# Scores of an attention branch with the query's two float halves stacked on the partitions

## The reference, cut to what matters

```python
def swa_sink_attention(q, k, v, sinks):
    qc = q.reshape(b, nc, CHUNK, A_KV_HEADS, g, d)
    kb, vb = chunk_band(k, n_prev), chunk_band(v, n_prev)
    logits = jnp.einsum('bnqhgd,bnkhd->bnhgqk', qc, kb) * (d ** -0.5)
    logits = jnp.where(valid[None, :, None, None, None, :], logits, -jnp.inf)
    probs = jax.nn.softmax(jnp.concatenate([logits, sink], axis=-1), axis=-1)[..., :-1]
    out = jnp.einsum('bnhgqk,bnkhd->bnqhgd', probs, vb)
```

## Time and profile before

| | us |
|---|---|
| median of three runs (lowest, highest) | 1487.55 (1487.49, 1489.11) |
| the profiled execution's own time | 1488.57 |
| its span, first to last instruction | 1486.6 |
| TensorE products busy | 1473.5, 7022 instructions |
| TensorE weight loads busy | 1215.9 |
| VectorE busy | 975.7 |
| ScalarE busy | 665.9 |
| score products of branch A (lines 662 to 664) | 26.9, 96 instructions |

### The profile page before, as it was taken

One profiled execution on the slowest core, in us unless ns is written; L12 is line 12 of the kernel. 1 busy time (PEld: TensorE's weight loads), 2 busy tenths in 40 slices (PEclk: granted clock), 3 DMA queues, 4 the chain that ended last, 5 costly groups with the idle time before them and its releaser, 6 DMA issues.

```text
span 1486.6 us, 19540 instructions
## 1 busy us (share of the span) xinstructions
PE 1473.5 (99%) x7022; PEld 1215.9 (82%) x7022; DVE 975.7 (66%) x1614; ACT 665.9 (45%) x1140; POOL 45.1 (3%) x35
## 2 busy tenths in 40 slices
PE   8999999999999999999999999999999999999998
PEld 6888888888888888888878888888888888888886
DVE  7777666565687734776477876665647776357753
ACT  6655555444444422443475555544345443234434
POOL 0000000002100000000200000000030000000001
PEclk9999999999999999999999999999999999999999
DMA  6222222232332233332432222222333332333331
GB/s 231 88 83 71 85 71 73 71 93 78 128 99 91 83 99 110 99 93 71 134 116 89 66 86 78 65 78 80 98 103 95 99 95 82 101 105 98 99 105 66
DMA packets 42560, 139.61 MB, mean 94 GB/s; under 512 B 5364, under 2 KB 5492, under 8 KB 42232
## 3 DMA queue, kind: packets, MB, share of 16 engines
q1 hardware_dynamic: 41760, 137.13, 29.3%
q10 hardware_dynamic: 728, 1.52, 0.3%
HBM read 136.53 MB, written 2.10 MB: 93 GB/s over the span
## 4 chain that ended last, share of the span: by engine, by line
PE 96%; ACT 1%; DVE 1%; DMA 1%; issue 1%; ACTq 0%; SPq 0%; DVEq 0%
PE dense L630 28%; PE dense L632 28%; PE dense L631 28%; PE turned L695 2%; PE branch L722 1%; PE dense L875 1%; PE dense L874 1%; PE dense L873 1%; DMA h<-in_x 1%; PE scores L683 1%; PE scores L682 1%; PE branch L708 1%; PE scores L686 0%; ACT tmp L1093 0%; ACT whi L943 0%
## 5 line engine op out<-in xcount | busy, mean ns | idle before, releaser
L630 PE MATMUL dense<-hg,whi 128*128 128x512 f32 x1376 | 547.7, 398 | 3.0 <-DVE hg L1285 2.6
L632 PE MATMUL dense<-hg,wlo 128*128 128x512 f32 x1376 | 537.4, 391 | 0.0
L631 PE MATMUL dense<-hg,whi 128*128 128x512 f32 x1376 | 537.0, 390 | 0.0
L943 ACT ACTIVATE whi<-raw 128x1024 fp32r<-128x1024 f32 (+3 forms) x269 | 265.4, 987 | 439.1 <-PE dense L632 417.5
L1272 DVE TENSOR_TENSOR wlo<-raw,whi 128x1024 fp32r<-128x1024 f32 (+3 forms) x269 | 305.9, 1137 | 180.2 <-ACT whi L943 177.9
L630 PEld LDWEIGHTS dense<-hg,whi 128*128 128x128 f32 x1376 | 259.6, 189 | 58.3 <-issue 4.8
L632 PEld LDWEIGHTS dense<-hg,wlo 128*128 128x128 f32 x1376 | 258.8, 188 | 55.0
L631 PEld LDWEIGHTS dense<-hg,whi 128*128 128x128 f32 x1376 | 259.4, 189 | 51.7 <-issue 1.0
L630 PE MATMUL dense<-act,whi 128*128 128x512 f32 x528 | 207.2, 393 | 0.0
L632 PE MATMUL dense<-act,wlo 128*128 128x512 f32 x528 | 205.6, 389 | 0.0
L631 PE MATMUL dense<-act,whi 128*128 128x512 f32 x528 | 205.5, 389 | 0.0
(11 more groups left out here) (188 smaller groups left out, 1269.8 us busy)
## 6 DMA issues: line engine op xcount, KB each, us to landing
raw<-in_w_up SPq DMA_DIRECT2D x88, 512.0 KB, 3.5
raw<-in_w_gate SPq DMA_DIRECT2D x48, 512.0 KB, 3.5
raw<-in_w_in SPq DMA_DIRECT2D x35, 512.0 KB, 3.5
raw<-in_w_down SPq DMA_DIRECT2D x32, 384.0 KB, 3.0
raw<-in_w_out SPq DMA_DIRECT2D x16, 512.0 KB, 3.4
raw<-in_w_down SPq DMA_DIRECT2D x16, 320.0 KB, 2.9
raw<-in_w_down_last SPq DMA_DIRECT2D x10, 512.0 KB, 3.5
raw<-in_w_br_a SPq DMA_DIRECT2D x8, 512.0 KB, 3.4
```

The source lines that it names most:

```text
L630: mm(out, a, xhi, start=start, stop=False)
L631: mm(out, a, xlo, start=False, stop=False)
L632: return mm(out, b, xhi, start=False, stop=stop)
L943: fn(whi[:, s, 0:cols], raw[:, r, 0:cols], ACT.Copy).then_inc(w_hi.sem, 1)
```

## The change

The first branch goes over to the stacked form. For each of a pair's two heads, `qa_st(g, s)` now holds the high half on the 64 partitions of head s and the low half on the other 64. The key is stored for each key head with the same 64 rows on both halves of the partitions, hi and lo, without zeros, by the "k" items that branches B and C have. A step is, for each key head s, two products of 128 columns (stacked q with k hi, stacked q with k lo), four in all, each head writing its own 128 columns of the bank. The first group of `SPLIT_QK` has eight items (four of q, four of k) in place of four, the second four in place of two, all of 64 partitions and 512 columns. All four partial products are now summed, lo x lo too.

```diff
-SPLIT_QK = [[("qa", 0, 0, 0), ("qa", 1, 0, 0), ("ka", 0, 0, 0), ("ka", 0, 1, 0)], [("qa", 2, 0, 0), ("qa", 3, 0, 0)]]
+SPLIT_QK = [[("qa", c, s, s) for c in range(2) for s in range(2)]
+            + [("k", 0, s, to) for s in range(2) for to in (s, 1 - s)],
+            [("qa", c, s, s) for c in range(2, 4) for s in range(2)]]
...
-    return SPLIT_QK[p][j:j + 1] if p < GROUPS else []
+    return SPLIT_QK[p][j:j + 1] if 0 < p < GROUPS else []
...
-        def qa_st(g, part):
-
-            return act2[:, 2 * g + part].rearrange("p i n -> p (i n)")
-
-        def qa_rows(p, part):
-
-            return qa_st(p // 2, part).rearrange("p (c i n) -> p c i n", i=2, n=CHUNK)[:, :, p % 2, :]
+        def qa_st(g, s):
+
+            return act2[:, 2 * g + s].rearrange("p i n -> p (i n)")
+
+        def qa_rows(p, s, r):
+
+            return qa_st(p // 2, s).rearrange("p (c i n) -> p c i n", i=2, n=CHUNK)[r, :, p % 2, :]
...
-                b = pair(bank_s[i % 2][:, 0:2 * P])
                 k0 = window(c)
-                q_hi, q_lo = [qa_st(g, part)[:, c * P:(c + 1) * P] for part in range(2)]
-                k_hi, k_lo = [ka_st[:, :, part, k0:k0 + P] for part in range(2)]
-                mm(b, q_hi, k_hi, start=True, stop=False)
-                mm(b, q_hi, k_lo, start=False, stop=False)
-                mm(b, q_lo, k_hi, start=False, stop=True).then_inc(scores.sem, 1)
+                for s in range(2):
+                    b, a = bank_s[i % 2][:, s * P:(s + 1) * P], qa_st(g, s)[:, c * P:(c + 1) * P]
+                    mm(b, a, ka_st[:, s, 0, k0:k0 + P], start=True, stop=False)
+                    last = mm(b, a, ka_st[:, s, 1, k0:k0 + P], start=False, stop=True)
+                last.then_inc(scores.sem, 1)
...
                 if kind == "qa":
-                    fn(qa_rows(c, 0), q[:, c, :].rearrange("p (c n) -> p c n", n=CHUNK), ACT.Copy).then_inc(qk_hi.sem, 1)
-                elif kind == "ka":
-                    fn(ka_st[:, s, 0, :], k[:, 0, :], ACT.Copy, scale=own_half[:, s:s + 1]).then_inc(qk_hi.sem, 1)
+                    fn(qa_rows(c, s, r), q[r, c, :].rearrange("p (c n) -> p c n", n=CHUNK),
+                       ACT.Copy).then_inc(qk_hi.sem, 1)
...
                 if kind == "qa":
-                    ve.tensor_tensor(qa_rows(c, 1), q[:, c, :].rearrange("p (c n) -> p c n", n=CHUNK),
-                                     qa_rows(c, 0).bitcast(F32), ALU.subtract).then_inc(qk_lo.sem, 1)
-                elif kind == "ka":
-                    ve.scalar_tensor_tensor(out=ka_st[:, s, 1, :], in0=k[:, 0, :], scalar=own_half[:, s:s + 1],
-                                            in1=ka_st[:, s, 0, :].bitcast(F32),
-                                            op0=ALU.mult, op1=ALU.subtract).then_inc(qk_lo.sem, 1)
+                    other = slice((1 - s) * HD, (2 - s) * HD)
+                    ve.tensor_tensor(qa_rows(c, s, other), q[r, c, :].rearrange("p (c n) -> p c n", n=CHUNK),
+                                     qa_rows(c, s, r).bitcast(F32), ALU.subtract).then_inc(qk_lo.sem, 1)
```

## The result

The changed kernel takes 1495.30 us (median of 6, 1494.16 to 1498.05), the kernel before beside it 1487.97 (median of 6, 1487.49 to 1489.11): a ratio of 1.0050, 95% interval 1.0039 to 1.0062, or 7.3 us between the medians. The profiled execution took 1495.56.

The account below looks back on a forecast made before the run. TensorE, busy 99% of the span, was taken as the bound; layer 0 at 4.5 and layer 1 at 2.15 us gave +6.6 on 1487.55, so 1494.1 us. The 8-in-10 range was 1491.3 to 1496.8.

Parts of the forecast that it names:

- Products: In 32 branch A steps, four products of 128 columns at 0.114 us, set by weight loads, replace three of 256: +2.5 us.
- Splits: Before step 0, eight VectorE low halves at 0.72 us each stop TensorE: +3.1 us in layer 0, +0.87 in layer 1.
- Rival (a): Before step 0, all eight splits cost 0.60 us, cheaper than held: sum +4.6, 1492.1 us; chance 0.10.
- (b): The splits before step 0 are covered and only the products count: +2.5, 1490.0 us; chance 0.05.
- (c): Columns set a product's price, so A steps shrink by 0.11 to 0.13 us: sum +1.4, 1489.0 us; chance 0.06.
- (d): TensorE is freed in the 32 A steps, at 0.11 us a step: -3.6, 1484.0 us; chance 0.02.
- Rival (e): The clock falls to 1.2 GHz in layer 0's stall of 3.1 us: +2.6 on top, 1496.7 us; chance 0.09.
- dense products of 0.63 behind the stall: Sign that the forecast is wrong: dense products behind layer 0's stall last 0.63 us, where elsewhere they last 0.39.
- What is late next: Work queued behind the splits moves later: unit 9's low-half weights come 3.5 us later in layer 0, TensorE's wait grows 0.1.
- The wait before unit 9: TensorE's wait in layer 0 for unit 9's low-half weights, 0.36 us before, forecast to grow by 0.1, between 0.3 and 0.6.
- nearly: In layer 1, unit 9's weights land at 801.0 and TensorE arrives at 801.3: no wait, but nearly.

Follow-up runs that it names:

- six-product kernel: The kernel before with each branch A score product of 256 columns cut into two of 128, splits untouched: 1497.39 us, ratio 1.0062.
- reordered list: The changed kernel with the first group's eight split items reordered so that more neighbours start in the same half: 1494.73 us, ratio 1.0045.
- filled stop: The changed kernel with 13 unread products of 512 columns before TensorE's wait at layer 0's first score step: 1495.11 us, ratio 1.0043.
- both edits: The changed kernel with its eight splits reordered and ScalarE's high halves issued before the forget branch's in unit 6: 1492.32 us, ratio 1.0028.
- two wide products: The changed kernel with two score products of 256 columns a step in place of four of 128: 1490.28 us, ratio 1.0016.

## Why the prediction was right, and where it was not

The time of 1495.3 lies 1.2 above the forecast and inside the range. Of the 1.2, 0.4 is the kernel before itself (1487.97 here, 1487.55 in the runs shown before), and 0.7 the change (7.3 for 6.6).

**Products.** Right: the number of loads and not of columns sets the price. More loads for the same columns cost 9.1 us, fewer gave 0.17 a step back. That it is the load, and not another price of each product that follows the clock, is likely from the rows and not shown by itself. The term came out at 2.4 for 2.5: 0.09 to 0.11 for steps followed by dense products (forecast 0.10), some 0.07 for the rest (0.075). The Trainium skill, "TensorE: Matmul & The Clock Gate", section "LDWEIGHTS (loading the stationary operand)", gives P/1.2 ns for P columns of weights, worked out 107 ns for 128, and all 64 of L664, 0.11 apart, agree; its "Back-to-back issue gap" would have them 56 ns apart (some 81 in a stream of loads and products), which the 128 products of L664 and L665 in the six-product kernel, at 275 to 277 ns and 0.11 apart, do not show either.

**Splits.** Right, to 0.02 us: 0.72 each by their neighbours' halves, a stop of 3.09 in layer 0, where there was no slack, and 0.85 in layer 1, where there were 2.35 us. Rival (a), all eight at 0.60, is excluded by the list's own distances, and the reordered list shows both prices in one row of eight. Rivals (b), (c) and (d) fell with these two.

**The clock.** This is the step that failed. Rival (e) happened, at a chance of 0.09, and with the wait that it hid it is the only part of the account that is off by more than 0.05. The forecast had named dense products of 0.63 behind the stall as a sign of being wrong, and they came. The rival's mechanism was named and its evidence read from the right rows: a stop longer than any in the kernel before. But having written that the stop lay outside everything the trace showed, I gave it one chance in eleven; there was no row against it, only none for it. Its price was off too. I took half of a stretch of 5.3 us, from the start-up; the fall lasts 3.4 us and costs 1.6, a full microsecond less than the 2.6. What the forecast gives without a fall can be read from the filled stop, where there was none: 6.5 by the trace, for 6.6. That the time with the fall lies so near is in part luck, since a third of the fall's cost was taken up by the next point, which the forecast did not have.

**What is late next.** The wait before unit 9 was to grow from 0.36 to 0.5 and it vanished: the half clock slowed TensorE by 1.6 while the weights' chain on VectorE and ScalarE, which that clock doesn't touch, went on (the low half of unit 8's weights lasts 1.22 in the low stretch, as elsewhere). So the net price of the fall is 1.6 less the 0.5 that would have been waited, 1.05. Where the clock stayed up the wait was there as forecast: 0.50 in the reordered list, 0.52 with the stop filled, 0.45 and 0.50 with both edits. In layer 1 of the changed kernel no wait appeared ("nearly", the forecast said), nor in unit 10; with cheaper products it did, 0.17 and 0.52.

**In the experiments** two expectations missed in what they say of a cause: the two wide products (0.22 a step for 0.17), and the clock at a stop of 1.9 us. The totals were also too low by 0.6 to 0.8 for the filled stop, the reordered list (without a fall) and both edits (5.8, 4.7 and 3.6 for 6.5, 5.5 and 4.2). Some 0.5 of each is that I had reckoned from 7.1 for the changed kernel, the difference of the spans, in which a start-up shorter by 0.5 is contained.

## What to carry to other kernels

Count weight loads, not columns, when products of 128 columns are exchanged for products of 256, or the other way round: here each load more cost about 0.09 us although no column was added. (Products of 512 columns stand 0.23 apart, so there the columns count.) Where a list of half-height VectorE instructions stands on the path, put those that start in the same half next to each other. And when a change opens a stop on TensorE that is longer than any in the trace, price the fall of the clock behind it as likely, read from the trace for how long the engines behind are covered by it, and consider another order of work, or even unused products, before the wait.

## What the runs showed of the hardware that I had not expected

- The clock falls behind the stop and not in it: 1.00 over 57.8 to 60.7, then 0.51 from 61.9 to 65.4. It fell after stops of 3.1, 2.6 (once in three) and 1.9 us, for 3.4 us each time, and each fall cost some 1.6 us of TensorE.
- Thirteen products of 512 columns in the stop kept the clock up in the one execution profiled, and were worth 1 us by the trace.
- A half clock on TensorE can hide another engine's lateness: the wait before unit 9 is 0.36 before, 0.45 to 0.52 behind a stop without a fall, and 0 behind one with it.
- On ScalarE too, copies of 64 partitions that change halves stand 0.65 apart, where the kernel before's two of 128 stood 0.52 apart; that had been the estimate, and it is hidden behind VectorE's 0.72. In the reordered list both occur on ScalarE as well: 0.52 to 0.54 behind a copy in the same halves, 0.64 to 0.65 behind one in others. Layer 0, ScalarE of the changed kernel:

```profile
54.44 2.58 ACT L1028 ACTIVATE act<-q 64x512 fp32r<-64x512 f32 x4
57.04 2.59 ACT L1033 ACTIVATE act<-k 64x512 fp32r<-64x512 f32 x4
```
